# Expert tokens in and out as rows through DRAM, in place of gather and scatter products, in a two-layer hybrid transformer on one Trainium2 core

## The reference, cut to what matters

```python
def _swiglu(x, w1, w3, w2):
    return (jax.nn.silu(x @ w1) * (x @ w3)) @ w2

def _moe(x, router, w1, w3, w2):
    logits = (x @ router).astype(jnp.float32)
    top_val, top_idx = lax.top_k(logits, TOP_K)
    weights = jax.nn.softmax(top_val, axis=-1)
    combine = jnp.sum(jax.nn.one_hot(top_idx, N_EXPERTS, dtype=jnp.float32) * weights[..., None], axis=-2)
    out = combine[..., 0:1] * _swiglu(x, w1[0], w3[0], w2[0])
    for e in range(1, N_EXPERTS):
        out = out + combine[..., e:e + 1] * _swiglu(x, w1[e], w3[e], w2[e])
    return out
```

## Time and profile before

| | us |
|---|---|
| median of 3 runs | 2292.59 (2292.26 to 2294.9) |
| the profiled execution, its own time | 2292.8 |
| its span in the profile | 2291.0 |
| PE busy | 2192.1 (96%) |
| DVE busy | 1439.9 (63%) |
| ACT busy | 1145.9 (50%) |
| POOL busy | 121.4 (5%) |
| chain that ended last, share of PE | 90% |
| HBM read / written | 443.59 MB / 2.10 MB |

### The profile page before, as it was taken

How to read it: one execution, slowest core, us unless ns; L and a number is a source line. 1 busy time by engine, 2 the same in 40 slices (tenths; PEclk the granted TensorE clock), 3 DMA queues, 4 the chain that set the end, 5 groups by cost and what they waited for, 6 DMA issues and landing times.

```text
span 2291.0 us, 37640 instructions
## 1 busy us (share of the span) xinstructions
PE 2192.1 (96%) x15678; PEld 1799.7 (79%) x15678; DVE 1439.9 (63%) x2102; ACT 1145.9 (50%) x1579; POOL 121.4 (5%) x94
## 2 busy tenths in 40 slices
PE   6999899999989999998997899999999999999998
PEld 4887687777778888886876899778888888888886
DVE  3556663334242222337565666499999989999998
ACT  3253433222242222324444354377877878787787
POOL 0013500000000000000035100000000000000000
PEclk9999999999999999999989999999999999999999
DMA  6400036565422222222200254288989999898995
GB/s 246 189 1 1 3 120 242 233 271 223 164 97 96 106 92 92 92 76 74 74 1 2 100 216 176 82 333 338 368 338 350 358 350 356 332 372 341 348 360 210
DMA packets 63180, 448.17 MB, mean 196 GB/s; under 512 B 7200, under 2 KB 8096, under 8 KB 9376
## 3 DMA queue, kind: packets, MB, share of 16 engines
q1 hardware_dynamic: 61008, 435.84, 49.7%
q10 hardware_dynamic: 2000, 9.88, 1.1%
HBM read 443.59 MB, written 2.10 MB: 195 GB/s over the span
## 4 chain that ended last, share of the span: by engine, by line
PE 90%; DVE 4%; ACT 3%; issue 2%; DMA 1%; POOL 1%; DVEq 0%; SPq 0%; ACTq 0%; PEldq 0%; POOLq 0%
PE bank L1236 12%; PE bank L1346 11%; PE bank L695 9%; PE bank L676 7%; PE bank L678 7%; PE bank L677 7%; PE bank L1354 5%; PE bank L1278 4%; PE bank L868 4%; PE bank L525 4%; PE bank L821 3%; PE bank L833 2%; PE bank L1258 2%; PE bank L720 2%; PE bank L614 1%
## 5 line engine op out<-in xcount | busy, mean ns | idle before, releaser
L2227 DVE TENSOR_TENSOR wsp_l<-ring,wsp_h 128x1024 fp32r<-128x1024 f32 x528 | 640.1, 1223 | 39.5 <-ACT wsp_h L1460 8.2
L1460 ACT CAST wsp_h<-ring 128x1024 fp32r<-128x1024 f32 x528 | 555.2, 1054 | 149.9 <-PE bank L678 88.7
L676 PE MATMUL bank<-wsp_h,xTs_h 128*128 128x512 f32 x704 | 283.7, 403 | 0.0
L678 PE MATMUL bank<-wsp_h,xTs_l 128*128 128x512 f32 x704 | 275.6, 391 | 0.0
L677 PE MATMUL bank<-wsp_l,xTs_h 128*128 128x512 f32 x704 | 274.4, 390 | 0.0
L2787 DVE TENSOR_TENSOR dsp_l<-ring,dsp_h 128x1024 fp32r<-128x1024 f32 x66 | 80.8, 1225 | 240.1 <-ACT dsp_h L1902 240.1
L1902 ACT CAST dsp_h<-ring 128x1024 fp32r<-128x1024 f32 x66 | 69.1, 1048 | 256.1 <-PE bank L1346 181.6
L1236 PE MATMUL bank<-u_hi,gsp_h 128*128 128x512 f32 (+1 forms) x512 | 174.2, 340 | 0.0
L1236 PE MATMUL bank<-x_lo,gsp_h 128*128 128x512 f32 (+1 forms) x512 | 171.9, 336 | 0.0
L1236 PE MATMUL bank<-u_hi,gsp_l 128*128 128x512 f32 (+1 forms) x512 | 171.5, 335 | 0.0
L678 PEld LDWEIGHTS bank<-wsp_h,xTs_l 128*128 128x128 f32 x704 | 132.2, 188 | 29.1
(11 more groups left out here) (372 smaller groups left out, 4261.4 us busy)
## 6 DMA issues: line engine op xcount, KB each, us to landing
ring<-in_moe_tiles_dram SPq DMA_DIRECT2D x264, 1024.0 KB, 4.9
ring<-in_ada_tiles_dram SPq DMA_DIRECT2D x48, 1024.0 KB, 9.3
ring<-in_ffn_tiles_dram SPq DMA_DIRECT2D x33, 1024.0 KB, 4.8
ring<-in_gate_tiles_dram SPq DMA_DIRECT2D x32, 1024.0 KB, 6.2
ring<-in_in_tiles_dram SPq DMA_DIRECT2D x22, 1024.0 KB, 4.8
arena<-in_branch_tiles_dram ACTq DMA_DIRECT2D x8, 1024.0 KB, 7.4
ring<-in_out_tiles_dram SPq DMA_DIRECT2D x8, 1024.0 KB, 4.9
h<-in_x_dram SPq DMA_DIRECT2D x2, 1024.0 KB, 6.0
```

The costliest lines, as they stand in the source:

```text
L676: pe.matmul(o, xTs[0][:, kk, :], whi[:, k, :], start=(kk == 0), stop=False)
L678: mm = pe.matmul(o, xTs[1][:, kk, :], whi[:, k, :], start=False, stop=(kk == KD - 1))
L1460: act.copy(wsp[0][:, g % 4, :], half_slot(MOE0, g)).then_inc(s.gq_o.up, 1)
L2227: v.tensor_tensor(wsp[1][:, g % 4, :], half_slot(MOE0, g), wsp[0][:, g % 4, :], ALU.subtract).then_inc(s.gq_pt.up, 1)
```

## The change

Tokens no longer reach the experts 1 to 7 through a product with a selection matrix. They are written once, as rows of 4 KB, to a DRAM tensor `x_dram` with 128 rows for each expert, and each expert's 128 rows are read back as one plain transfer. Results of the experts 0 to 6 are written as rows to `y_dram`, and each token's two rows are read back at the end.

- **SP, layer 0.** After the last w_in load it writes a zero tile (`nil`) over seven blocks of `x_dram` and over the last two of `y_dram`: 4.5 MiB in two DMAs. DVE waits for them ahead of the attention of layer 0, since `nil` lies in memory that is used there.
- **POOL.** It zeroes `nil` at the start. Once the ranks are known it works out, in 11 small instructions, each token's two row numbers (`place_of`), then writes the rows with four indirect DMAs of 128 rows each (`x_put`), waits for these and for the seven result transfers, and reads the rows back with four indirect DMAs (`y_got`).
- **ACT.** Its first four roundings of weights stand ahead of the branch and wait for no other engine. In each expert but the last it issues the read of the next expert's rows at block 32 (in expert 0 after a wait for `x_put`), and in each but the first the write of the last expert's results at block 4. `selection` is left for the last expert alone.
- **PE.** Expert 0 keeps a gather by product, now of 16 plain float32 matmuls. For the experts 1 to 7 there are 8 transposes of the rows (`row_transposes`). `scatter` is gone, `sel_transposes` stays in the last expert.
- **DVE.** The split of the tokens (`vns_l`), six of eight `select`s, all `accumulate`s and the `y_lo` of seven experts are gone; a `select` has two instructions. In the last expert four instructions of 1024 elements each (`combine`) weigh and add the rows read back. They wait for `y_got`.

```diff
+                if n == WIN_SLOT[0][-1]:
+                    sp.wait_ge(*sig[0].pad_ok(1))
+                    sp.dma_start(x_dram[P:NE * P, :].rearrange("(e p) n -> p e n", p=P),
+                                 nil.unsqueeze(1).to_broadcast([P, NE - 1, D])).then_inc(nil_out.semaphore, 16)
+                    sp.dma_start(y_dram[(NE - 1) * P:, :].rearrange("(e p) n -> p e n", p=P),
+                                 nil.unsqueeze(1).to_broadcast([P, 2, D])).then_inc(nil_out.semaphore, 16)
...
-                def gather(e):
-
-                    pe.wait_ge(*a.m_sel(e + 1))
-                    if e:
-                        pe.wait_ge(*a.m_hTs(NF // 2 * e))
+                def gather():
+
+                    pe.wait_ge(*a.m_sel(1))
                     for k in range(KD):
-                        for q, (t, part) in enumerate(((0, 0), (0, 1), (1, 0), (1, 1))):
+                        for t in range(2):
                             mm = pe.matmul(bank[2 + k // 4][:, P * (k % 4):P * (k % 4 + 1)],
-                                           vns[part][:, t, P * k:P * (k + 1)], sel_r[:, t, :],
-                                           start=(q == 0), stop=(q == 3))
+                                           vn[:, t, P * k:P * (k + 1)], sel[:, t, :], start=(t == 0), stop=(t == 1))
                     mm.then_inc(s.gq_max.up, 1)
 
+                def row_transposes(e):
+
+                    pe.wait_ge(*x_back(16 * e))
+                    pe.wait_ge(*a.m_hTs(NF // 2 * e))
+                    for k in range(KD):
+                        mm = transpose(bank[2 + k // 4][:, P * (k % 4):P * (k % 4 + 1)], x_rows[:, P * k:P * (k + 1)])
+                    mm.then_inc(s.gq_max.up, 1)
...
-                        if c == 0:
+                        if c == 0 and e == NE - 1:
                             sel_transposes()
-                            if e:
-                                scatter(e - 1)
...
                         if f == 8 and e + 1 < NE:
-                            gather(e + 1)
+                            row_transposes(e + 1)
...
-                for g in range(4):
-                    high(g)
                 act.wait_ge(*s.gq_max(1))
                 tokens_high()
                 for e in range(NE):
                     for q in range(4, SPLITS + 4):
                         if SPLITS * e + q < SPLITS * NE:
-                            high(SPLITS * e + q)
+                            expert_weight_high(s, SPLITS * e + q)
+                        if q == 4 and e:
+                            act.wait_ge(*a.m_y(e + 1))
+                            act.dma_start(y_dram[P * (e - 1):P * e, :], y_rows).then_inc(y_kept.semaphore, 16)
+                        if q == 32 and e + 1 < NE:
+                            if e == 0:
+                                act.wait_ge(x_put, 64)
+                            act.dma_start(x_rows, x_dram[P * (e + 1):P * (e + 2), :]).then_inc(x_back.semaphore, 16)
...
                     if e < NE - 1:
                         act.wait_ge(*used(SPLITS * (e + 1) + 4))
-                        act.copy(ysp[0][:, 0:512], bank[4][:, :])
-                        act.copy(ysp[0][:, 512:D], bank[5][:, :]).then_inc(a.m_y.up, 1)
+                        if e:
+                            act.wait_ge(*y_kept(16 * e))
+                        act.copy(y_rows[:, 0:512], bank[4][:, :])
+                        act.copy(y_rows[:, 512:D], bank[5][:, :]).then_inc(a.m_y.up, 1)
...
+            pool.wait_ge(*moe.m_y(1))
+            for j in range(4):
+                pool.indirect_dma_start(x_dram, rows_at(j), vn[:, j % 2, :], None).then_inc(x_put, 16)
+            pool.wait_ge(x_put, 64)
+            pool.wait_ge(*y_kept(16 * (NE - 1)))
+            for j in range(4):
+                pool.indirect_dma_start(y_back_rows[:, j, :], None, y_dram, rows_at(j)).then_inc(y_got, 16)
...
-                def accumulate(e):
-
-                    v.wait_ge(*a.f_out(e + 1))
-                    for t in range(2):
-                        for hf in range(2):
-                            c = slice(512 * hf, 512 * (hf + 1))
-                            ins = v.scalar_tensor_tensor(macc[:, t, c], bank[(6, 4)[t] + hf][:, :],
-                                                         comb[:, t, e + 1:e + 2], macc[:, t, c], ALU.mult, ALU.add)
-                    ins.then_inc(a.f_acc.up, 1)
+                def combine(n):
+
+                    t, c = n % 2, n // 2
+                    v.wait_ge(y_got, 64)
+                    share = small[:, 190 - 2 * c + t:191 - 2 * c + t]
+                    if c == 0:
+                        link(v.tensor_scalar(macc[:, t, :], y_back_rows[:, t, :], share, None, ALU.mult))
+                    else:
+                        link(v.scalar_tensor_tensor(macc[:, t, :], y_back_rows[:, 2 + t, :], share, macc[:, t, :],
+                                                    ALU.mult, ALU.add))
...
+                        if e == NE - 1 and q in (28, 32, 36, 40):
+                            combine(q // 4 - 7)
...
+                if l == 0:
+                    v.wait_ge(*nil_out(32))
```

More of the change, by code:

```diff
@@ L630, in last_scatter @@
                             mm.then_inc(a.f_out.up, 1)
-                def scatter(e):
-                    pe.wait_ge(*a.m_y(e + 2))
-                    pe.wait_ge(*a.y_low(e + 1))
-                    pe.wait_ge(*a.m_sT(e + 1))
-                    pe.wait_ge(*a.f_acc(e + 1))
-                    for t in range(2):
-                        for hf in range(2):
-                            for x in range(2):
-                                mm = pe.matmul(bank[(6, 4)[t] + hf][:, :], selT[:, t, :], ysp[x][:, 512 * hf:512 * (hf + 1)],
-                                               start=(x == 0), stop=(x == 1))
-                    mm.then_inc(a.f_out.up, 1)
                 def sel_transposes():
+                    pe.wait_ge(*a.m_sel(2))
                     for t in range(2):
@@ L1437, in dense_experts_act, with expert_weight_high @@
                         act.activation(sil[:, f % 2, 0:SEQ], bank[f % 2][:, 0:SEQ], ACT.Silu).then_inc(s.f_sil.up, 1)
+            def expert_weight_high(s, g):
+                n = MOE0 + g // 2
+                act.wait_ge(slot_full[n % RING], 16 * (n // RING + 1))
+                if g >= 4:
+                    act.wait_ge(*s.gq_s(g + 1))
+                act.copy(wsp[0][:, g % 4, :], half_slot(MOE0, g)).then_inc(s.gq_o.up, 1)
             def sparse_experts_act(s):
@@ L1971, in _ @@
                         for q in range(2):
-                            ins = act.copy(vns[0][:, t, 512 * q:512 * (q + 1)], bank[2 + 2 * t + q][:, :])
+                            ins = act.copy(vn[:, t, 512 * q:512 * (q + 1)], bank[2 + 2 * t + q][:, :])
                     ins.then_inc(moe.m_y.up, 1)
+                    for g in range(4):
+                        expert_weight_high(again, g)
                     act.wait_ge(*s.rcomb(4))
@@ L2275, in sparse_experts_dve @@
                                 hidden(e, c)
[L2276 to L2281 removed]
+                            if r == 3 and c == 0 and e == NE - 2:
+                                select(NE - 1)
                         if q == 2 * NF + 5:
@@ L2900, in _ @@
                 v.wait_ge(*moe.m_y(1))
-                for t in range(2):
-                    for q in range(2):
-                        c = slice(512 * q, 512 * (q + 1))
-                        ins = v.tensor_tensor(vns[1][:, t, c], bank[2 + 2 * t + q][:, :], vns[0][:, t, c], ALU.subtract)
-                link(ins)
                 select(0)
```

99 lines of the change are left out of this document (54 added, 45 removed).

## The result

| | before | after |
|---|---|---|
| median | 2292.43 (2288.95 to 2294.9, 4 runs) | 2257.81 (2256.44 to 2261.43, 4 runs) |
| ratio to before | 1 | 0.9849, 95% interval 0.9834 to 0.9864 |
| profiled execution, span | 2291.0 | 2254.6 |
| one expert (from result copy to result copy) | 98.83 | 93.87 |

The forecast was 2258.9, with a range of 2253.5 to 2271.0. The time lies 1.1 us under it. What follows is about whether it came out so for the stated reasons, and two of the terms did not.

A forecast was written before the change was run, and what follows sets the result against it. PE was taken to bound the experts block after block. Savings of 18.55 + 12.95 + 1.5 + 1.2 less 0.3 made 33.9 us, and 2292.8 - 33.9 = 2258.9 us, with a range of 2253.5 to 2271.0.

The forecast's parts named there:

- PE is the bound: Expert stage: PE, busy 98.73 of 98.80 us, decides the time if DVE and DMA keep up; chance 0.66.
- Tokens in: PE in seven experts: 8 transposes (0.87 us) replace the 3.52 us gather, saving 2.65 each, 18.55 us in all.
- late block: PE's one block delayed behind DVE's burst in each expert, 0.40 us against 0.23: seven times 0.17, 1.2 us saved.
- Results out: PE: the 1.85 us scatter gone seven times, 12.95 us, and two `sel` transposes of 0.22 us, 1.5 us.
- DVE: In each expert about 5 us of work leaves DVE, mostly worth nothing; it keeps about 7 us of room in 94.
- combine: Last expert: four DVE instructions over 16 blocks cost PE between 0 and 2 us, taken as 0.3.
- The head: Start of the experts: `select(0)` ends 2.9 us earlier, costed at nothing; 16 float32 matmuls take as long as the 32.
- The rival with a chance of 0.11: Start of the experts: earlier `select(0)` brings 2.9 us, or the half clock partly goes; 2254 to 2256 us, chance 0.11.
- POOL: Index work some 4 us, then four indirect DMAs of 512 KB taking 20 us (10 to 48), hidden with 10 us or more.
- DMA: Expert stage: rows raise the load to 35.65 MB an expert, 379 GB/s in 94.0 us; delay hidden, costed at nothing.
- Both DMA rivals: Expert stage: DMA limit 370 GB/s gives 2276 us, chance 0.08; limit 356 GB/s gives 2302 us, chance 0.04.
- The zeros: Layer 0: 4.7 MB written from 104 us take 17 us, hidden with 33 us of room before DVE's wait.

The follow-up runs named there:

- e1: Tokens' half of the change alone, results still by scatter, `y_lo` and `accumulate` as in the kernel before: 2269.8 us, ratio 0.9902, expert 95.98 us.
- e2: Results' half of the change alone, each expert's tokens gathered by 16 float32 matmuls: 2276.3 us, ratio 0.9923 to the kernel before, expert 96.57 us.
- e5: Changed kernel with the four `combine` instructions moved behind DVE's last low part: 2255.3 us, ratio 0.9853 to the kernel before, last expert 90.2 us.
- e3: Changed kernel with the four `combine` instructions moved to blocks 50 to 62 of the last expert: 2260.0 us, ratio 0.9847, last expert 91.2 us.
- e9: Changed kernel with `combine`'s multiplications and additions on POOL instead of as extra DVE work: 2259.8 us, ratio 0.9879, last expert 94.4 us.
- e4: Changed kernel with the old gather of 32 fp32r matmuls in expert 0: 2262.0 us in one run, records to first block 13.85 us.
- e11: Kernel before with expert 0's gather as 16 float32 matmuls of the high parts only: 2289.8 us, ratio 0.9996, records to first block 11.55 us.
- e10: The changed kernel run once more, unaltered, in a later group: 2254.9 us, ratio 0.9859 to the kernel before, expert 93.87 us.
- e8: Changed kernel with ten extra unused 512 KB reads in each of experts 1 to 6: 2266.7 us in one run, expert 95.87 us.

## Why the prediction was right, point by point

- *PE is the bound*: right. 93.95 of 94.00 us busy, ACT's waits on PE's lines alone. An expert of 93.87 for 94.0 forecast (93.94 by the terms; PE loses 4.89 us by them, not 4.8).
- *Tokens in, 2.65*: mis-sized by a little. By the rows 3.52 - 0.80 = 2.72: eight transposes with matmuls behind them take 0.80 us of the stream, not the 0.87 of a run in the chain. e1's 2.85 is this and most of a late block of 0.17.
- *Results out, 1.85 + 0.22, and the late block, 0.17*: right, 2.26 in e2.
- *DVE*: its cover was right, the size was not. In the stretch shown DVE is busy 88.3 us in 94, where 86 to 87 were expected. Over the experts 1 to 6 its busy time fell from 92.0 to 88.15 us an expert, 3.9 and not 5, though the records that left add up to 5.1. Records that follow each other on DVE overlap by nearly 0.1 us, so they count for less in busy time than in their sum; whether that is all of it isn't shown. DVE's room is 5.7 us in an expert, not 7, and most of it lies in short gaps for which the profile names no releaser: it waits for ACT only 7.2 us in six experts. This is what the next term ran into.
- *combine, 0.3 in bounds of 0 to 2*: the step that failed, though inside its bounds. It was sized by the burst of `accumulate`, 2.72 us for 0.17 of PE. But four instructions of together 4.0 us (two of 0.75 and two of 1.28) in 16 blocks stand against DVE's room in those 16 blocks. In an expert's first part DVE is busy 19.23 of 20.00 us (1720 to 1740), in its last 22 blocks 12.79 of 14.00 (1744 to 1758): by an estimate from these, a room of 0.9 us in 16 blocks of the first part and of 1.9 in 16 of the last. What is over, 3.1 and 2.1 us, must come out of the `wsp` buffers that are filled ahead and then out of PE's stream. Against e5, the first placement cost 1.7 us and the second (e3) 1.0, so about half of what is over was paid by PE. The sum of the instructions against the room in their stretch was the rule to use, and the nearest row was not.
- *The head, 0 in bounds of 0 to 2.9*: the part on `select` was right (gather 4.99 us after the records, 4.81 before). The step that failed is "the 16 float32 matmuls should take as long as the 32". At full clock they do, 3.65 us for 3.52. But they also keep the clock behind the wait, worth 1.8 us. The rival with a chance of 0.11 had the half clock partly gone, from a shorter gap; it came, from another cause.
- `combine` cost 1.4 us more than its term and the head gained 1.8 more than its own: the two errors cancel, which is luck. That the time came out 1.1 us off says little by itself too: the same kernel's second median is 3 us lower, and the profiled execution gained 36.4 us of span for the 33.9 forecast, 1.3 of them ahead of the experts.
- *ACT's issues, nothing*: right, no trace of them in the waits.
- *POOL, 20 us for the four*: right for the reads, too high for the writes. The index work is ten instructions, not eleven, and took 3.9 us. The four reads of the last expert took from 2150.4 to 2171.1 in e9, 20.7 us, beside a full stream of weights. The four writes were issued from 1484.76 to 1488.80 and landed 3.7 us after their issue by the median, in a stretch with a DMA share of 0.55: about 8 us for the four, an estimate from these rows. POOL itself is held 0.95 to 1.7 us for each indirect DMA. The cover was about 10 us for the reads (`combine` starts at 2185.3) and near 40 for the writes. That DVE would run little but tensor_tensor beside both sets was wrong for the writes: DVE stood idle for 6.69 us until 1488.68. It holds for the reads, and they did not starve: 1.04 to 1.66 us of POOL each.
- *DMA, nothing*: right. 385 GB/s, weights landing in 7.0 us. Both DMA rivals fall: their limits of 370 and 356 were taken from stretches in which no more was asked for.
- *The zeros*: hidden, landed 16 to 18 us after their issue at 104 and 105 us, some 30 us ahead of the row that waits.

## What to carry to other kernels

Where one engine is the bound block after block, what leaves its stream comes back in full, and the row of the chain with its start times is the right price; check first that the next engines have room for the shorter period. For work that is added beside such a stream, hold its sum against the room of its engine in that very stretch, not against the room of the whole stage; here about half of what was over came out of the stream, in both placements tried. And don't take a DMA share near 1 for a full queue: the rate under an added load, or the landing time, tells the room.

## What the hardware showed that I had not expected

- The kind of a product of 128 columns moved TensorE's clock: 32 fp32r products brought the granted clock from 1.0 to 0.54, the level of 1.2 GHz, 16 float32 ones (32 records) in the same 3.7 us left it at 1.0, on the level of 2.4 GHz, with the same wait ahead (down in the kernel before and in e4; kept in the changed kernel, e11, and e1 to e10 without e4). With no wait ahead the fp32r products kept it too (the kernel before, experts 1 to 7).
- An indirect DMA of 128 rows of 4 KB holds POOL for 0.95 to 1.7 us, and DVE's low parts beside the reads keep their 1.22 us (DVE was idle beside most of the writes).
- POOL's own arithmetic on SBUF does hold up DVE: low parts of 1.22 us took up to 3.43 beside it.
- One core carries 425 to 427 GB/s over a whole stage of 575 us (e8, one run), with a DMA share that reads 0.98 at 385 and 1.00 to 1.01 from 402 on.
